# A new order, a slot of its own for the first y, deferred x loads and a second PSUM class for the last z in an eight-core decoder trunk

## The chip, the cores and the metric

The kernel runs on the eight cores of one Trainium2 chip. Each core works on its own share of the batch with no exchange between cores. The metric is the device time in microseconds (us) of the slowest core. TensorE, VectorE (DVE), ScalarE (ACT), GpSimd (POOL) and SyncE (SP) of a core each run their own instruction stream in order and meet at semaphores. POOL and SP also issue the transfers.

## The reference

Two layers, each on x with 1024 channels. A layer normalises x, multiplies by one wide input weight whose columns are seven groups, works on two head groups and adds an output product:

```
h  = rmsnorm(x, g)
a_val, a_gate, z_a, Bg, C, hb, z_b = split(h @ w_in)      # 7 x 1024 columns
u  = a_val * sigmoid(a_gate)                              # group A
ca = head_layernorm(causal_dwconv(u, width 31) + bias)    # per head of 128 channels
y_a = silu(ca) * silu(z_a)
v  = C * hb                                               # group B
y_b = Bg * causal_dwconv(v, width 3) * silu(z_b)
x  = x + concat(y_a, y_b) @ w_out                         # 2048 -> 1024
```

After layer 2 there is a final rmsnorm. Outputs are the x of the prompt and the samples, and the last rows of the inputs of both convolutions for every layer. The batch has 8 prompts of 2048 positions and 128 samples of 4 new positions.

## The kernel before, in words

Each core takes one prompt and 16 samples: 2112 columns, in four blocks of 512 (0 to 3) and block 4 of 64. Channels lie on partitions, x and h in eight chunks of 128. All products run on TensorE, with 128 x 128 weights against 512 (or 64) columns.

Per layer the work is split by head j: **P** is the GLU pair (value and gate), **C** the convolution of width 31 as Toeplitz matmuls (L1102, L1103) followed by the layer norm, **Z** the gate z_A, **a** the product C * hb of group B, **b** its gates Bg and z_B. ORDER lists them for each layer. "Z7up" is a Z whose y lies in a slot of the up_sb tile.

A product of two weight tiles over the four big blocks runs in one of two ways. *plain* makes eight times four matmuls for two weight tiles and two blocks. *pair* (line 984) is a Strassen-like scheme: seven products of four matmuls for the same, with sums of the weights (wsum) and of h (in xst) made beforehand, and copies and differences in PSUM (L1004, L1017) between them. STEPSP, STEPSa and STEPSb are the orders of these steps. WK lists the products of each layer that run as pairs; of those that it names, P0, P1 and a0 run block by block in the first loop all the same.

The first loop (line 1543 on) goes block by block through P0, P1 and a0, since block q's h only exists once x of that block has come and its squares are summed: rms_stat (line 763) squares on ACT (L783), either adds chunk pairs on DVE (L791) or, for the blocks in DIRECT, lets TensorE sum all chunks with a matrix of ones, and then goes through Ln (L806) and Exp (L820) on ACT and the h products on DVE (L869). Blocks 0 and 1 of layer 0 are RAW: they start on x that isn't normalised and are finished later (raw_finish, L850 and L852). In the rows this matrix is ones_s, the squares are tmp, and psb is any PSUM bank.

The convolution of head 0 needs u of P0: it is stored to DRAM (scr_u, L1045), read back in another layout (up_sb, L1060) and needs the last columns of the neighbour group (the halo copies on POOL, L1043) beforehand. The layer norm goes through DRAM too (scr_c, L1146, L1149). The last product of a layer is out_final: 16 tiles of w_out (256 KB each) are loaded by POOL into slots that earlier work frees, as HOMES gives them; output blocks come in the order OUTQ (in layer 1: block 4 of 64 columns, then 0, 1, 2, 3), each summed over 16 chunks of y in PSUM, then added to x on DVE (L1358). In layer 1 x comes back from x_mid in DRAM through SP (L1332). PSUM banks are shared by classes, CAPS: five for "proj", two for "conv", one for "z".

The order of the instructions is not written by hand. A list scheduler (class Sched) takes all operations with their resources, keys (BG shifts these by name), pools and PSUM classes, and writes an order for each engine, which the engines then follow. Weight tiles for products wait in a pool of slots (wsl). y has a pool of its own. x of the first loop lies in an area ("arena") in y_sb and xst, and a y may be written there once its readers are through.

Lines in the text are those of the profile of the kernel before. The matmul helper is L743, that of the pairs L996. In the new kernel the same lines are L748, L1001, and later ones move by 5 to 18.

Of the kernel before, what the change touches and what calls it, by code (L numbers as in the profile page):

```python
# [30 lines left out]
NB = 5  # L31
# [16 lines left out]
    "b0 C0 a1 C1 P2 C2 Z0 b1 P3 a2 Z1 P4 C3 C4 P5 Z2 b2 P6 a3 C5 b3 C6 Z3 P7 a4 Z4 Z5 b4 Z6 a5 C7 b5 a6 b6u0 a7 b7u1 Z7up",  # L48
    "b0 C0 a1 C1 P2 Z0 b1 C2 Z1 P3 a2 P4 C3 C4 P5 b2 Z2 P6 a3 b3 C5 Z3 a4 C6 Z4 Z5 b4 P7 a5 C7 b5 a6 b6 a7 Z6u0 b7u1 Z7up",
# [20 lines left out]
WK = ['P0 P1 P2 P3 P4 P5 P6 a0 a2 a3 a4 a5 a6 a7 b6 b7', 'P0 P1 P2 P3 P4 P5 P6 P7 a0 a1 a2 a3 a4 a5 a6 a7 b6 b7']  # L70
BG = {"sd": -300, "p5b": 30, "co": 30, "y": 300, "sz": -30, "halo": 30, "sdb": 100, "th": -30, "sub": -300, "c": 30, "s": 30, "sa": 100, "hist": -30, "wt": 30, "nrm": -30, "p": -300, "lsq": -300, "sb": -300, "u2": -30}
# [432 lines left out]
def build_nc():  # L504
# [35 lines left out]
    def sb(name, shape, dt):  # L540
# [222 lines left out]
    def rms_stat(part, pool=False, after=(), early=False, copy=False, raw=False, direct=False):  # L763
# [4 lines left out]
        for kp in range(4):  # L768
            s = V("snap")
            if q in SPLIT and raw and kp == 3:  # L770
# [553 lines left out]
    def x_stage(l, q):  # L1324
# [4 lines left out]
        for i, v in enumerate(x.vs):  # L1329
# [177 lines left out]
    for l in range(DEPTH):  # L1507
# [213 lines left out]
```

How the kernel before makes its waits and increments, by code:

```python
            def body(e):  # L482
                for o in self.order[name]:
                    for d in o.waits:
                        e.wait_ge(chan_sems[d.chan] if d.chan is not None else sems[d.eng], d.cnt)
                    ins = o.fn(e)
                    if o.chan is not None:
                        ins.then_inc(chan_sems[o.chan], 16)
                    elif o.sig:
                        ins.then_inc(sems[name], 1)
                if name == "sp":
                    for ch in final_chans:
                        if ch in cnt:
                            e.wait_ge(chan_sems[ch], cnt[ch])
```

## Time and profile before

| what | value |
|---|---|
| median of 3 runs | 1088.03 us (1087.13 to 1253.58) |
| the profiled execution | 1088.93 us, span 1087.4 us on the slowest core, core 7 |
| spans of all cores | 1078.9 to 1087.4 us, granted clock 0.995 to 0.998 |
| TensorE busy | 1054.1 us, 97% of the span, 7010 instructions |
| DVE, ACT, POOL busy | 751.3 us (69%), 630.0 us (58%), 311.0 us (29%) |
| bytes by DMA | 142.45 MB, mean 131 GB/s |

The profile was taken on the slowest core. A span runs from the first to the last instruction. What lies outside it is 1.5 us. TensorE's granted clock is in tenths or parts of its full speed (2.4 GHz); 0.50 is the lower of its two levels.

### The profile page before, as it was taken

What the parts mean: (1) busy time and instruction counts of PE and PEld (TensorE: products, weight loads), DVE (VectorE), ACT (ScalarE), POOL (GpSimd) and SP (SyncE); (2) the same over time, 40 slices, a digit from 0 to 9 for tenths busy, and PEclk for the clock granted to TensorE, in tenths of its full rate; (3) what the DMA queues carried; (4) which work ended last, traced back from release to release, by engine and by line L of the source; (5) the groups of instructions that cost most, each with busy time, mean ns of one, the idle gap of its engine ahead of it and who ended that gap; (6) DMA issues with size and microseconds to landing.
All of it is one profiled execution on the core that took longest, in us unless ns stands there. A gap on an engine that the chain in (4) does not pass through costs nothing.

```text
span 1087.4 us, 21321 instructions; the slowest of 8 cores (1078.9 to 1087.4 us)
## 1 busy us (share of the span) xinstructions
PE 1054.1 (97%) x7010; PEld 528.3 (49%) x7010; DVE 751.3 (69%) x1458; ACT 630.0 (58%) x1029; POOL 311.0 (29%) x470
## 2 busy tenths in 40 slices
PE   6989999999999999999999999999999999989997
PEld 3445455555544544444544445545455554444464
DVE  3768978778688887433555888788779788843332
ACT  5954777686777665121151568768577866533332
POOL 7462222222232222222151222222312222213341
PEclk9989999999999999999999999999999999999999
DMA  9927878869676759554433775885966765931454
GB/s 238 206 28 141 129 135 120 150 101 158 114 118 114 115 99 200 146 186 177 158 99 89 114 125 92 154 157 87 154 107 96 140 110 79 203 97 35 146 154 169
DMA packets 185803, 142.45 MB, mean 131 GB/s; under 512 B 140000, under 2 KB 152160, under 8 KB 185632
## 3 DMA queue, kind: packets, MB, share of 16 engines
q0 software_dynamic: 34352, 54.97, 33.8%
q1 hardware_dynamic: 150816, 82.17, 30.5%
q10 hardware_dynamic: 528, 3.96, 1.0%
q8 instruction: 58, 0.95, 0.4%
q14 instruction: 49, 0.40, 0.2%
HBM read 149.08 MB, written 43.79 MB: 177 GB/s over the span
## 4 chain that ended last, share of the span: by engine, by line
PE 90%; DMA 5%; POOL 1%; ACT 1%; issue 1%; DVE 1%; ACTq 0%; DVEq 0%; SPq 0%; POOLq 0%
PE psb L743 55%; PE psb L996 31%; DMA wsl<-w_in_r 2%; PE psb L1102 2%; PE psb L1103 2%; PE psb L1441 1%; DMA wsl<-w_out_r 1%; DMA big<-scr_c 1%; DMA scr_c<-big 1%; DMA xst<-x_mid 1%; POOL y_sb L1480 0%; DMA y_fm<-xst 0%; POOL toep L1521 0%; POOL wsl L722 0%; PE psb L1444 0%
## 5 line engine op out<-in xcount | busy, mean ns | idle before, releaser
L743 PE MATMUL psb<-h_sb,wsl 128*128 128x512 bf16 (+1 forms) x2272 | 364.4, 309 | 10.9 <-DVE h_sb L869 3.2
L743 PEld LDWEIGHTS psb<-h_sb,wsl 128*128 128x128 bf16 x2272 | 167.6, 98 | 181.5 <-issue 19.3
L1076 ACT ACTIVATE toep<-wt_sb 32x512 bf16<-32x512 bf16 x192 | 119.8, 625 | 33.5 <-PE psb L1103 21.5
L1358 DVE TENSOR_TENSOR xst<-xst,psb 128x512 f32<-128x512 f32 (+2 forms) x80 | 44.7, 566 | 123.5 <-PE psb L743 99.8
L783 ACT ACTIVATE tmp<-xst 128x1024 bf16<-128x1024 f32 (+2 forms) x44 | 38.6, 880 | 150.6 <-DVE xst L1358 140.9
L1285 DVE SCALAR_TENSOR_TENSOR tmp<-vbuf,cw_b_sb,tmp 128x512 f32<-128x512 bf16 (+1 forms) x160 | 108.0, 675 | 19.7 <-ACT tmp L1282 11.5
L996 PE MATMUL psb<-h_sb,wsl 128*128 128x512 bf16 x448 | 113.6, 379 | 0.4 <-ACT psb L1004 0.4
L996 PE MATMUL psb<-xst,wsum 128*128 128x512 bf16 x448 | 110.8, 379 | 1.3 <-DVE wsum L950 0.8
L996 PE MATMUL psb<-h_sb,wsum 128*128 128x512 bf16 x448 | 108.8, 379 | 1.0 <-DVE psb L1017 1.0
L722 POOL DMA_DIRECT2D wsl<-w_in_r x110 | 60.0, 552 | 166.9 <-PE psb L743 91.6
L1069 POOL DMA_DIRECT2D wt_sb<-wt_d x64 | 35.2, 551 | 214.1 <-DVE toep L1080 68.1
L791 POOL TENSOR_TENSOR tmp<-tmp 128x512 bf16<-128x512 bf16 (+2 forms) x40 | 37.4, 935 | 160.4 <-ACT tmp L783 160.3
L1282 ACT ACTIVATE tmp<-vbuf,cw_b_sb 128x512 f32<-128x512 bf16 (+1 forms) x80 | 51.4, 642 | 35.6 <-DVE y_sb L1315 30.1
L1107 DVE TENSOR_TENSOR big<-psb,cbt_sb 128x320 bf16<-128x320 f32 x128 | 62.3, 487 | 13.0 <-PE psb L1103 10.8
L1197 ACT ACTIVATE tmp<-big,vecs_sb 128x512 f32<-128x512 bf16 (+1 forms) x80 | 58.8, 735 | 19.9 <-DMA big<-scr_c 6.5
L743 PE MATMUL psb<-h_sb,wsum 128*128 128x512 bf16 (+1 forms) x288 | 68.3, 369 | 0.0
L743 PE MATMUL psb<-y_sb,toep 128*128 128x512 bf16 (+2 forms) x320 | 67.0, 333 | 0.0
L996 PEld LDWEIGHTS psb<-xst,wsum 128*128 128x128 bf16 x448 | 41.9, 98 | 48.0 <-issue 2.5
L743 PE MATMUL psb<-y_sb,wsl 128*128 128x512 bf16 (+2 forms) x280 | 59.9, 327 | 3.8 <-DMA wsl<-w_out_r 3.8
L996 PEld LDWEIGHTS psb<-h_sb,wsum 128*128 128x128 bf16 x448 | 41.3, 98 | 45.3 <-issue 2.1
L996 PEld LDWEIGHTS psb<-h_sb,wsl 128*128 128x128 bf16 x448 | 40.8, 98 | 42.8 <-issue 1.0
L743 PE MATMUL psb<-y_sb,wsum 128*128 128x512 bf16 (+2 forms) x280 | 60.6, 335 | 0.2 <-issue 0.2
(155 smaller groups left out, 1826.8 us busy)
## 6 DMA issues: line engine op xcount, KB each, us to landing
wsl<-w_in_r POOLq DMA_DIRECT2D x110, 256.0 KB, 5.7
scr_u<-u_sb SPq DMA_DIRECT2D x16, 704.0 KB, 6.8
up_sb<-scr_u SPq DMA_DIRECT2D x16, 704.0 KB, 7.5
scr_c<-big SPq DMA_DIRECT2D x16, 640.0 KB, 7.2
big<-scr_c SPq DMA_DIRECT2D x16, 640.0 KB, 6.1
wt_sb<-wt_d POOLq DMA_DIRECT2D x64, 128.0 KB, 4.0
xst<-x_d SPq DMA_DIRECT2D x16, 512.0 KB, 8.5
x_mid<-xst SPq DMA_DIRECT2D x16, 512.0 KB, 2.9
```

Of the source, the lines that this page charges most:

```text
L722: return e.dma_start(out=wsl[:, v.slot, :], in_=src)
L743: ins = e.matmul(bank(v, n), lhsT=l_(), rhs=r_(), start=(first and i == 0), stop=(last and i == len(pairs) - 1))
L783: act((lambda e, s=s, kp=kp: e.activation(out=tmh(s, 0, 2 * n).rearrange("p (k c) -> p k c", k=2), in_=x2(kp, part), func=AF.Square)), 2 * ...
L791: S.op("pool" if pool else "dve", (lambda e, s=s: e.tensor_tensor(out=tmh(s, 0, n), in0=tmh(s, 0, n), in1=tmh(s, n, n), op=ALU.add)), 0.15 ...
L996: ins = e.matmul(bank(v, 512), lhsT=lhs(k), rhs=rhs(k), start=first and k == 0, stop=True if not first else k == 3, skip_group_check=not f ...
L1069: pooldma((lambda e: e.dma_start(out=wt_sb[:, w.slot, :], in_=wt_d[l, j, qt])), 0.75, (), [w], f"wt{(j * 4 + qt) % 4}", pkt=0.09, name=f"w ...
L1076: act((lambda e, p=p, c=c: e.activation(out=toep[p, tp.slot, :].rearrange("p (m x) -> p m x", x=128)[:, :, 32 * c:32 * c + 32], in_=wt_sb[ ...
L1107: dve((lambda e, b=b, v=v, bias=bias: e.tensor_tensor(out=big[:, co.slot, 4 * b:4 * b + 4, :], in0=bank(v, 4 * CROW).rearrange("p (g c) -> ...
L1197: act((lambda e, s=s, q=q, n=n: e.activation(out=b4(tm(s, n), q), in_=c_blk(cn.slot, q), func=AF.Silu, scale=vecs[:, 16 + col:17 + col], b ...
L1282: act((lambda e: e.activation(out=b3(tm(a, n), q), in_=v_blk(q, 0), func=AF.Copy, scale=cw_b[:, l, j, 2:3])), n, [v_r[q], cwb_r], [a], ptr ...
L1285: dve((lambda e, lag=lag: e.scalar_tensor_tensor(out=b3(tm(a, n), q), in0=v_blk(q, lag), scalar=cw_b[:, l, j, 2 - lag:3 - lag], in1=b3(tm( ...
L1358: x_op[0] = dve((lambda e: e.tensor_tensor(out=x.s(m, part), in0=x.s(m, part), in1=bank(v, n), op=ALU.add)), n, [v, xr], [xr], holds=x.hol ...
```

## The change

ORDER, the step orders, the order of output blocks, of z blocks, and the scheduler's key offsets (BG) and the lists of pairs (WK) are replaced by others. Block 3 joins DIRECT: TensorE sums its squares. In layer 1 a0 leaves the first loop (FIRST) and becomes a pair in its ORDER. The first y of b0 gets a slot "e" of its own in y_sb that nothing of x uses; the pool of y has one slot less and x of block 4 moves to xst. In the last layer the x loads of the second output block (block 0) also wait for the last four w_out tiles of the list (XLW): two in wsum and two in big. The five z products of Z7 take their PSUM banks alternately from the classes z and conv. START puts w3 ahead of the x load of block 4, and w6 ahead of that of block 3.

```diff
--- before.py
+++ after.py
@@ -45,20 +45,20 @@
 ORDER = [
...
-    "b0 C0 a1 C1 P2 Z0 b1 C2 Z1 P3 a2 P4 C3 C4 P5 b2 Z2 P6 a3 b3 C5 Z3 a4 C6 Z4 Z5 b4 P7 a5 C7 b5 a6 b6 a7 Z6u0 b7u1 Z7up",
...
+    "C0 P1 a0 Z0 b0 a1 C1 P2 C2 Z1 P3 b1 a2 C3 P4 b2 P5 C4 Z2 Z3 P6 a3 b3 C5 C6 a4 Z4 P7 b4 Z5 C7 a5 b5 a6 Z6 b6u0 a7 b7u1 Z7up",
...
-STEPSb = "P11 P51 P50 P61 P10 P60 P20 P31 P71 P30 P21 s P41 P70 P40"
...
+STEPSb = "P10 P50 P11 P60 P51 P61 P20 P31 P71 s P21 P30 P41 P70 P40"
...
-OUTQ = (1, 2, 0, 4, 3)
+OUTQ = (0, 4, 2, 1, 3)
...
-ZQ = (2, 1, 4, 3, 0)
+ZQ = (3, 2, 0, 4, 1)
@@ -67,17 +67,20 @@
-WK = ['P0 P1 P2 P3 P4 P5 P6 a0 a2 a3 a4 a5 a6 a7 b6 b7', 'P0 P1 P2 P3 P4 P5 P6 P7 a0 a1 a2 a3 a4 a5 a6 a7 b6 b7']
+WK = ['P0 P1 P2 P3 P4 P5 P6 a0 a2 a3 a4 a5 a7 b0 b3 b6 b7', 'P0 P1 P2 P3 P4 P5 P6 P7 a0 a1 a2 a3 a4 a6 a7 b4 b7']
...
-DIRECT = (0, 1, 2, 4)
-
-START = "u0 u1 t0 t1 w0 w1 x1 w2 x4 w3 x2 w4 w5 x3 w6 w7"
+DIRECT = (0, 1, 2, 3, 4)
+
+FIRST = (('P0', 'P1', 'a0'), ('P0', 'P1'))
+XLW = 4
...
+START = "u0 u1 t0 t1 w0 w1 x1 w2 w3 x4 x2 w4 w5 w6 x3 w7"
...
-FINISH = {2: (0,), 3: (1,)}
+FINISH = {1: (0,), 4: (1,)}
@@ -583,7 +586,7 @@
-        "y": Pool(NY, spare=1),
+        "y": Pool(NY - 1, spare=1),
@@ -1167,6 +1172,8 @@
+            if self.place == "e":
+                return y_sb[:, NY - 1, a:b]
@@ -1175,9 +1182,10 @@
-    def proj_t(w, zs, q, **kw):
-        v = V("bank", "z", "full")
+    def proj_t(w, zs, q, cls="z", **kw):
+        v = V("bank", cls, "full")
@@ -1191,16 +1199,17 @@
-        for q in ZQ if j == 7 else range(NB):
+        for i, q in enumerate(ZQ if j == 7 else range(NB)):
             n = BLOCKS[q][1]
+            cls = "conv" if j == 7 and i % 2 else "z"
...
             if PAIRS and q in (1, 3):
-                bz = proj_t(w, zs, q, after=[cn_of[(l, j, "op")]], name=f"z{j}.{q}", **y.kw())
+                bz = proj_t(w, zs, q, cls, after=[cn_of[(l, j, "op")]], name=f"z{j}.{q}", **y.kw())
             else:
-                bz = proj(w, q, cls="z", after=[cn_of[(l, j, "op")]], name=f"z{j}.{q}", **y.kw())
+                bz = proj(w, q, cls=cls, after=[cn_of[(l, j, "op")]], name=f"z{j}.{q}", **y.kw())
@@ -1321,7 +1330,7 @@
-    def x_stage(l, q):
+    def x_stage(l, q, after=()):
@@ -1331,7 +1340,7 @@
                   1.9 * w / 1024, [] if l == 0 else [xmid_r[q][i]], x.res[2 * i:2 * i + 2] if q < 4 else x.res, f"xl{nx[0] % NX}",
-                  pkt=0.172 if q < 4 else 0.09, holds=[v], after=x_late if l == 0 else (), name=f"xl{q}.{i}")
+                  pkt=0.172 if q < 4 else 0.09, holds=[v], after=list(after) + (x_late if l == 0 else []), name=f"xl{q}.{i}")
@@ -1392,7 +1401,7 @@
             if part[1] == 0:
-                x_stage(l, part[0])
+                x_stage(l, part[0], [r.w for rr in wres[-XLW:] for r in rr] if final and n == 1 and XLW else ())
@@ -1511,7 +1520,7 @@
-            w_first = [w_load(w_in_r[l, c]) for c in (8, 0, 9, 1, 32, 40)]
+            w_first = [w_load(w_in_r[l, c]) for t, c in (("P0", 8), ("P0", 0), ("P1", 9), ("P1", 1), ("a0", 32), ("a0", 40)) if t in FIRST[l]]
@@ -1569,25 +1580,27 @@
-            y = Y()
+            y = Y("e")
...
-                y = Y(rest[1:] or None)
+                y = Y("e" if tok == "b0" else rest[1:] or None)
@@ -1605,7 +1618,7 @@
-            if not (tok == "b0" and w_b0):
+            if not (tok == "b0" and w_b0 or tok in w_of):
```


The new order at three places. The first is TensorE at the end of layer 0's first loop. Rows with ones_s sum the squares of block 3, the last in this loop. wsl holds weight tiles, wsum two of b0's weight tiles here. Before:

```order
L743 MATMUL psb<-h_sb,wsum 128x512 x8
L743 MATMUL psb<-h_sb,wsl 128x64 x24
L743 MATMUL psb<-tmp,ones_s 128x512
L743 MATMUL psb<-h_sb,wsum 128x512 x8
L743 MATMUL psb<-tmp,ones_s 128x512
L743 MATMUL psb<-h_sb,wsum 128x64 x16
L743 MATMUL psb<-h_sb,wsl 128x512 x48
L743 MATMUL psb<-h_sb,wsum 128x512 x48
L743 MATMUL psb<-h_sb,wsl 128x512 x20
L743 MATMUL psb<-h_sb,wsum 128x512 x4
```

Now:

```order
L748 MATMUL psb<-tmp,ones_s 128x512 x2
L748 MATMUL psb<-h_sb,wsl 128x512
L748 MATMUL psb<-h_sb,wsum 128x512 x16
L748 MATMUL psb<-h_sb,wsl 128x64 x8
L748 MATMUL psb<-h_sb,wsum 128x64 x8
L748 MATMUL psb<-h_sb,wsl 128x512 x2
L748 MATMUL psb<-h_sb,wsl 128x64 x8
L748 MATMUL psb<-h_sb,wsum 128x64 x8
L748 MATMUL psb<-h_sb,wsl 128x512 x46
```

Before, 16 matmuls of 64 columns stand between the last sum and the first products of block 3 (the row of 48). Now 17 of 512 columns and 16 of 64 stand there; then come the first two matmuls of block 3, 16 more of 64 columns, and the other 46.

The second is TensorE at the end of layer 1, from the last pair's matmuls (L996, in the new kernel L1001) on. The products from h_sb with zsum or wsl are z products (and some of block 4 of 64 columns); those from y_sb are the first output sums, of block 4, which read w_out tiles in toep, wsl and later slots. Before:

```order
L996 MATMUL psb<-xst,wsl 128x512 x4
L743 MATMUL psb<-y_sb,wsl 128x64 x4
L743 MATMUL psb<-y_sb,toep 128x64 x4
L743 MATMUL psb<-y_sb,wsl 128x64 x4
L743 MATMUL psb<-h_sb,wsl 128x64 x8
...
L743 MATMUL psb<-y_sb,wsl 128x64 x4
L743 MATMUL psb<-h_sb,wsl 128x512 x4
L743 MATMUL psb<-h_sb,zsum 128x512 x4
L743 MATMUL psb<-h_sb,wsl 128x512 x8
L743 MATMUL psb<-y_sb,wsl 128x64 x2
```

Now:

```order
L1001 MATMUL psb<-xst,wsl 128x512 x8
L748 MATMUL psb<-h_sb,wsl 128x512 x16
L748 MATMUL psb<-h_sb,wsl 128x64 x8
L748 MATMUL psb<-y_sb,toep 128x64 x4
L748 MATMUL psb<-y_sb,wsl 128x64 x4
...
L748 MATMUL psb<-y_sb,wsl 128x64 x4
L748 MATMUL psb<-h_sb,wsl 128x512 x4
L748 MATMUL psb<-h_sb,zsum 128x512 x4
L748 MATMUL psb<-y_sb,toep 128x64 x4
L748 MATMUL psb<-y_sb,wsl 128x64 x6
```

Behind the pair's last four matmuls there were 16 of 512 columns up to the row of y_sb, wsl x2, whose tile is the last one loaded; now there are 24, since the last two steps of the pair stand together ahead of 16 of them. The rows left out are of 64 columns.

The third is SP at the end of layer 1: the x loads (L1332, now L1341), the load of tail_d and the store of ob. Before:

```order
L1332 DMA xst<-x_mid 128x512
L1332 DMA xst<-x_mid 128x1024
L1614 DMA ob_d<-obt 128x272
L1332 DMA xst<-x_mid 128x1024 x2
L1409 DMA big<-tail_d 128x1152
L1332 DMA xst<-x_mid 128x1024 x2
L875 DMA y_fm<-xst 128x128 x4
```

Now:

```order
L1418 DMA big<-tail_d 128x1152
L1627 DMA ob_d<-obt 128x272
L1341 DMA xst<-x_mid 128x512
L1341 DMA xst<-x_mid 128x1024 x5
L880 DMA y_fm<-xst 128x128 x4
```

The load of tail_d and the store of ob come first now, and no x load stands between them.

## Rows read from the trace of the kernel before

**Rows 1.** The page's chain that ended last: share of the span by engine.

```profile
PE 90%; DMA 5%; POOL 1%; ACT 1%; issue 1%; DVE 1%; ACTq 0%; DVEq 0%; SPq 0%; POOLq 0%
```

**Rows 2.** Windows: stretch, length, busy us (instructions) of PE, PEld, DVE, ACT, POOL; clock; DMA.

```profile
0.00:70.00 70.00, 55.75 (x317) 26.45 (x318) 40.92 (x85) 52.58 (x77) 42.14 (x55) 0.95 0.71 173
70.00:945.00 875.00, 868.79 (x5909) 432.25 (x5907) 659.95 (x1277) 533.25 (x881) 229.69 (x374) 1.00 0.69 129
945.00:970.00 25.00, 18.51 (x196) 11.02 (x195) 13.59 (x29) 9.65 (x18) 2.64 (x8) 0.93 0.56 135
...
sum 1087.40, PE 1054.09 PEld 528.26 DVE 751.29 ACT 629.97 POOL 311.02; mean PE 263.52 PEld 132.06 DVE 187.82 ACT 157.49 POOL 77.76
```

**Rows 3.** Waits of TensorE: who waited for what; us in total, times, longest.

```profile
PE psb L743 <- DMA wsl<-w_out_r: 3.8, 1, 3.8
PE psb L743 <- DVE h_sb L869: 3.2, 1, 3.2
PE psb L743 <- ACT tmp L1205: 2.5, 2, 1.7
PE psb L743 <- DMA big<-scr_c: 1.6, 1, 1.6
```

**Rows 4.** Spans of the cores and their mean granted clock.

```profile
core 4: 1084.5 us, clock 0.997
...
core 7: 1087.4 us, clock 0.995
```

**Rows 5.** Timeline, first loop's end: start, busy us, engine, line, tiles, [idle before, releaser].

```profile
60.08 0.63 PE L743 MATMUL psb<-h_sb,wsum 128*128 128x64 bf16 x16
60.32 1.28 ACT L806 ACT_TABLE_LOAD   x1 [0.21 <-PE psb L743]
...
63.01 1.41 DVE L869 SCALAR_TENSOR_TENSOR h_sb<-xst,vecs_sb,psb 128x512 bf16<-128x512 f32 x2 [2.05 <-ACT psb L820]
...
63.91 0.59 PE L743 MATMUL psb<-h_sb,wsl 128*128 128x512 bf16 x1 [3.20 <-DVE h_sb L869]
```

**Rows 6.** Busy time in three short stretches, same columns.

```profile
60.00:65.00 5.00, 1.80 (x21) 0.94 (x19) 2.68 (x5) 4.67 (x7) 2.96 (x4) 0.80 0.00 0
65.00:70.00 5.00, 5.00 (x13) 1.78 (x12) 5.00 (x8) 4.28 (x8) 3.70 (x3) 0.52 0.01 3
960.70:964.10 3.40, 3.40 (x65) 3.40 (x66) 1.90 (x8) 0.62 (x2) 0.91 (x3) 0.50 0.02 5
```

**Rows 7.** Timeline of TensorE in the tail.

```profile
947.91 1.03 PE L996 MATMUL psb<-xst,wsl 128*128 128x512 bf16 x4
948.77 0.28 PE L743 MATMUL psb<-y_sb,wsl 128*128 128x64 bf16 x4
...
960.25 0.22 PE L743 MATMUL psb<-y_sb,wsl 128*128 128x64 bf16 x2 [3.76 <-DMA wsl<-w_out_r]
```

**Rows 8.** DMA issues of 944.2:949.6, then 933.9:934.55, 920.5:920.6: count, KB each, us to landing.

```profile
xst<-x_mid SPq DMA_DIRECT2D x2, 512.0 KB, 10.7
wsum<-w_out_r POOLq DMA_DIRECT2D x2, 256.0 KB, 11.5
wsl<-w_out_r POOLq DMA_DIRECT2D x1, 256.0 KB, 10.3
...
wsl<-w_out_r POOLq DMA_DIRECT2D x2, 256.0 KB, 6.9
...
wsl<-w_out_r POOLq DMA_DIRECT2D x1, 256.0 KB, 5.6
```

**Rows 9.** The first convolution: DMA issue on SP, its landing, TensorE's start.

```profile
85.88 0.37 SPq L1060 DMA_DIRECT2D up_sb<-scr_u  x1
...
up_sb<-scr_u SPq DMA_DIRECT2D x1, 704.0 KB, 7.5
...
97.90 0.20 PE L1102 MATMUL psb<-up_sb,toep 128*128 128x80 bf16 x1
```

**Rows 10.** DMA issues of 523.4:523.6, end of layer 0.

```profile
x_mid<-xst SPq DMA_DIRECT2D x1, 256.0 KB, 18.3
```

More of the change, by code:

```diff
@@ L625, in flat @@
                     return xst[:].rearrange("p a t -> p (a t)")[:, k * n:(k + m) * n]
-                lo = 4096 * self.q if self.q < 3 else 12288
+                if self.q == 4:
+                    return xst[:, 4, k * n:(k + m) * n]
+                lo = 4096 * self.q
                 return x0f[:, lo + k * n:lo + (k + m) * n]
@@ L783, in rms_stat @@
             act((lambda e, s=s, kp=kp: e.activation(out=tmh(s, 0, 2 * n).rearrange("p (k c) -> p k c", k=2), in_=x2(kp, part), func=AF.Square)),
-                2 * n, [xp(2 * kp, part), xp(2 * kp + 1, part)], [s], sbuf=True, tab=None, after=after, holds=hold(2 * kp), name=f"sq{q}.{kp}")
+                2 * n, [xp(2 * kp, part), xp(2 * kp + 1, part)], [s], sbuf=True, tab=None, after=after, holds=hold(2 * kp), name=f"{SI if x.first else 'sq'}{q}.{kp}")
             if direct:
@@ L1156, in __init__ @@
         def __init__(self, place=None):
-            self.res = rs(NB)
+            self.res = rs(NB) if place != "e" else e_r
             self.v = V("y") if place is None else None
             self.place = place
-            base = x0_arena if place is None else u_r[int(place[1])] if place[1] in "01" else [up_r, uph_r]
+            base = () if place == "e" else x0_arena if place is None else u_r[int(place[1])] if place[1] in "01" else [up_r, uph_r]
             self.after = [o for r in base for o in r.r + ([r.w] if r.w else [])]
-            if place is not None:
+            if place not in (None, "e"):
                 late_y[place] = self.res
@@ L1530, in build_nc @@
                     x_load(i, ("pool",))
-        wA, wB = w_first[:4], w_first[4:]
+        w_of = {t: (w_first[2 * i], w_first[2 * i + 1]) for i, t in enumerate(FIRST[l])}
         if l == 0:
@@ L1549, in build_nc @@
                 r = rms_stat(whole(nxt), after=[rms_stat.ln], raw=nxt in RAW, direct=nxt in DIRECT)
-            p1_block(l, 0, q, wA[0], wA[1], sp, cur)
-            p1_block(l, 1, q, wA[2], wA[3], sp, cur)
+            for j in range(2):
+                if f"P{j}" in w_of:
+                    p1_block(l, j, q, *w_of[f"P{j}"], sp, cur)
             if nxt in RAW:
@@ L1555, in build_nc @@
                 rms_apply(0, whole(nxt), r)
-            pb_a_block(l, 0, q, wB[0], wB[1], sp, cur)
+            if "a0" in w_of:
+                pb_a_block(l, 0, q, *w_of["a0"], sp, cur)
             if cur is not None:
@@ L1562, in build_nc @@
         if l == 0:
-            x0_arena[:] = [r for q in (0, 1, 2, 4) for r in xcur[q].res]
-            x_late[:] = [o for r in xcur[3].res for o in r.r + [r.w]]
+            x0_arena[:] = [r for q in (0, 1, 2) for r in xcur[q].res]
+            x_late[:] = [o for q in (3, 4) for r in xcur[q].res for o in r.r + [r.w]]
         else:
@@ L1571, in build_nc @@
             dve(lambda e: e.memset(vbuf[:, 0:2, :], 0.0), 160, (), [vh_r])
-        p1_end(l, 0)
-        p1_end(l, 1)
+        for j in range(2):
+            if f"P{j}" in w_of:
+                p1_end(l, j)
         up_load(l, 0)
-        pb_a_end(l, 0)
+        if "a0" in w_of:
+            pb_a_end(l, 0)
         pending = []
         if w_b0:
-            y = Y()
+            y = Y("e")
             pending.append((8, y))
@@ L1582, in build_nc @@
             t_forms(x_late)
-        seen = {"P0", "P1"}
+        seen = set(w_of)
         ups = [1]
@@ L1615, in build_nc @@
         last = l == DEPTH - 1
-        pending.sort(key=lambda cy: cy[1].v is None)
+        pending.sort(key=lambda cy: cy[1].place not in (None, "e"))
         assert len(pending) == 16
```

10 lines of the change are left out of this document (6 added, 4 removed).

## The prediction

> **What bounds the kernel now.** The chain of waits comes first [rows 1]: TensorE fills 90% of the span and DMA 5%, so time can be won almost only where TensorE stands idle or runs at half clock, or by taking matmuls out. The table by stretch [rows 2] tells how much that is: TensorE is busy 1054.1 of 1087.4 us. Of the 33.3 us of idle time 14.3 lie before 70 us, where the first x and weights arrive, 6.2 between 70 and 945, 6.5 in the 25 us after that. The list of waits [rows 3] names the ends of them: 3.8 us for a w_out tile, 3.2 for the h of block 3 (DVE L869), 2.5 for the SiLU of z (ACT L1205), 1.6 for the relayout of c. The spans of the cores [rows 4] say whose time counts: core 7's, 2.9 us longer than core 4's. The profiled execution took 1088.93 us, 1.5 more than its span and 0.9 more than the median of the runs (1088.03).
>
> **The change part by part.** The number of matmuls hardly moves: 28 products run as pairs before and after (the entries of WK that the first loop runs by block don't count), and the order has 7000 matmuls against 6996. The four more sum block 3's squares, which DVE L791 added before: 4 x 0.216 us = **+0.9** (four matmuls of 512 columns start at 947.91, the next group at 948.77 [rows 7], so 0.216 each; one of 64 columns is worth 0.0285).
>
> *The stall at the end of the first loop.* TensorE issues the last 16 matmuls of 64 columns at 60.08 and has nothing until 63.91 [rows 5], as the chain from the last sum of squares runs through a table load (60.32), Ln, Exp and DVE L869 (63.01): 3.83 us against 0.63 of matmuls. In the new order 17 matmuls of 512 columns and 16 of 64 stand between that sum and the first product that reads block 3's h: 17 x 0.216 + 16 x 0.0285 = 4.1 us. That covers the chain; but the h tiles come at DVE's 0.70 a tile (1.41 for two), and other work on DVE stands between them, which leaves some 0.7 of waiting: 3.2 - 0.7 = **-2.5**.
>
> *The clock behind it.* In 60 to 65 us the granted clock is 0.80 and in 65 to 70 it is 0.52 [rows 6]: TensorE ran at its 1.2 GHz level from about 64 to 70, directly behind the idle stretch. Six us at half clock cost 3.0. The fall follows the stall, so I take it back with it: **-3.0**, bounds 0 and -3.4 (0.68 x 5, both stretches).
>
> *The tail.* The last w_out tile goes into the slot that layer 1's last pair frees. The pair's last four matmuls start at 947.91, and the first matmul that needs the tile at 960.25, after a wait of 3.76 [rows 7]. The tile took 10.3 us, beside two x loads of 512 KB (10.7) [rows 8]. In the order before, 16 matmuls of 512 columns and 44 of 64 stand between the pair's end and that use, 4.7 us; now 24 and 48, 6.55. Also block 0's four x loads now wait for the two wsum tiles, so fewer loads share the DMA engines with the last one. In less crowded places the same transfer took 5.6 and 6.9 [rows 8]. With 0.7 from release to issue and 0.5 from landing to use, a tile of 5.6 is 0.2 us late, of 6.9 1.5, of 10.3 about 5. I take 0.2, since only the wsum pair and one x load are left beside it. The z stalls of 1.7 and 0.8 [rows 3] go too: the last z products now alternate between two classes of PSUM banks, so that one need not wait until the SiLU has emptied the other's; what is late next there is the SiLU itself, 0.5 at most. 3.76 + 2.5 - 0.2 - 0.5 = **-5.6**, ends -1.4 (tile as slow as before) and -6.3 (no wait left).
>
> By the Trainium skill ("DMA: Bandwidth & Descriptors", section Queues, rings and completion order) each DMA engine takes turns between the queues that have work. By that a tile that no longer shares with the x queue would land in half of 10.3, an estimate of 5.2, and the tail would give -5.8; the 5.6 of the less crowded row agrees with it, the 6.9 less so.
>
> The deferred x loads stay hidden. Issued when the wsum tiles land (11.5 us after an issue that comes 4.5 ahead of the pair's end), they are there 11.5 - 4.5 + 10.7 = 18 us after that end, 21 if each is 1.5 slower. TensorE stops for them only once five banks hold block 0's sums: 6.6 of cover, some 3 of 64-column sums and 5 x 16 x 0.216 = 17.3, together 26.
>
> *The clock in the tail* was 0.50 from 960.7 to 964.1 [rows 6], a loss of 1.7. It follows the longest wait there; **-1.5**, bounds 0 and -1.7.
>
> *The middle.* In layer 0 one z product waits 1.6 for its normalised c [rows 3], which goes through DRAM. By the order the fewest matmuls between the sums over a c and its z product are worth 16.1 us there, so the way takes 17.7; in the new order the fewest of all heads are worth 22.0: **-1.6**. The other small waits stay in kind, since one convolution and the next stand as close as before (13.1 us of matmuls, now 13.5).
>
> *The first convolution.* The relayout of u is issued at 85.88 and takes 7.5, so it landed at 93.4; the convolution starts at 97.90, a margin of 4.5 [rows 9]. The new order puts 91 matmuls of 512 columns between u's product and the convolution, not 111: 20 x 0.216 = 4.3 less, so the margin is gone; and POOL issues four weight loads, not three, ahead of the halo copies that the store of u waits for. Half a us for that issue and one for a fuller DMA: **+1.5**, between 0 and +5.1 (both transfers of u as slow as the 10.3 of [rows 8]).
>
> *At nothing.* Block 0's first y in a slot of its own: the last reader of x's arena, ACT L850, works in the first loop, and b0's products come after it. x of block 3 one weight tile later: its squares now end ahead of more matmuls than before. Layer 1's first loop without a0: the cover of each sum of squares falls from 32 to 22 us, still five times that chain [rows 5]. The store of ob and the load of tail_d change places with x loads on SP, and nothing on SP waits long for them.
>
> Sum: -2.5 - 3.0 - 5.6 - 1.5 - 1.6 + 0.9 + 1.5 = -11.8; 1088.9 - 11.8 = **1077 us**, for a profiled execution as for the runs within the 0.9 between them.
>
> **Rivals.** (1) *The tile's wait stays*, 14%: it needs 10.3 again and is 5 late, the clock falls behind it: 5.6 - 1.4 + 1.5 = 5.7 not won, 1083. For it speaks that the wsum tiles took 11.5 [rows 8]. (2) *The first loop's stall moves on*, 10%: TensorE waits 5 us for the first convolution instead of 1.5 and the clock falls there: 1077 + 3.5 + 3.0 = 1084. (3) *The middle gets new waits*, 10%: its idle time is 6.2 [rows 2] and the whole order is new; if it doubles, with 2 us of clock beside it, 1085. (4) *Slower*, 6%: u's relayout meets other transfers, as one of 256 KB took 18.3 us beside the copies of layer 0's end [rows 10], against 7.5 here. 10.8 later still, with 3.0 of clock: 1077 + 13.8 = 1091. It decides from 9 us of lateness beyond the sum's 1.5 on. Against it: nothing of such a copy runs near 90 us. (5) *No effect*, 5%: the pairs are 28 on both sides and the waits only change their names, 1088 to 1089. My forecast has 55%.
>
> A rule that speaks against the deferral stands in the Trainium skill, "DMA: Bandwidth & Descriptors", section Issuing engines are not separate DMA queues: all DMAs run on the same 16 engines, whoever issues them. By it the bytes of x are only moved; the price would be block 0's loads coming late, 18 to 21 us against the 26 above, so nothing.
>
> **Range and chances.** From 1070 (all bounds won, no wait at the convolution) to 1089 (rivals 1, 2, 3 and most of 5 inside). Faster by over 2%, about what a measurement of this kernel can tell from no change, needs less than 1066.3: 3%. Slower by 2% needs over 1109.8: 2%. Between: 95%.
>
> **What would show it.** After the change: no wait of TensorE for the h of block 3 over 1 us, and a clock of 1.00 from 60 to 70; the w_out wait under 1 us, with the last tile landing in 5 to 7; no wait for the relayout of c in the middle; 0 to 5 us of waiting for up_sb at the first convolution. I am wrong if that wait is over 5, if the last tile still needs 10, or if the idle time between 70 and 945 exceeds 12.

## The result, and the profile after

The changed kernel took 1075.99 us (median of 4 runs, 1075.59 to 1078.02) against 1088.03 us for the kernel before, run beside it (3 runs, 1087.13 to 1088.83): a ratio of 0.9893, 95% interval 0.9874 to 0.9913. Here and below, medians leave out the runs of a slower state that any of these kernels can fall into, in which a die's cores show a lower granted clock (1253.58 us for the kernel before). 1077 was forecast, with 1070 to 1089 as its range. The profiled execution took 1075.72 us; its slowest core is core 2 with 1074.2 us, core 7 follows with 1074.1. Since the rows of before are core 7's, those of after are taken from core 7 too, where nothing else is said.

The page's chain of waits, by engine, to be held against [rows 1]: the DMA share is down from 5% to 3%.

```profile
PE 89%; ACT 3%; DMA 3%; issue 2%; DVE 1%; POOL 1%; ACTq 0%; DVEq 0%; POOLq 0%; SPq 0%
```

The windows of core 7, columns as in [rows 2]:

```profile
0.00:70.00 70.00, 55.73 (x333) 26.61 (x334) 37.01 (x81) 51.16 (x75) 41.63 (x55) 1.00 0.71 173
70.00:945.00 875.00, 872.63 (x5962) 434.92 (x5961) 664.50 (x1289) 540.41 (x890) 230.05 (x376) 1.00 0.70 129
945.00:970.00 25.00, 24.76 (x200) 12.76 (x199) 12.16 (x31) 8.88 (x16) 6.50 (x9) 1.00 0.46 138
970.00:1074.10 104.10, 96.15 (x524) 51.69 (x522) 32.30 (x57) 31.23 (x49) 33.02 (x31) 0.98 0.44 132
```

Idle time of TensorE is length less busy. Before 70 us it is 14.3, as before, though the stall of 3.2 is gone from it; from 70 to 945 it is 2.4 in place of 6.2; in the 25 us behind that 0.2 in place of 6.5. Behind 970 us it has grown from 6.4 to 8.0; the row of the kernel before for this stretch, which [rows 2] leaves out, is:

```profile
970.00:1087.40 117.40, 111.04 (x594) 58.54 (x592) 36.84 (x69) 34.48 (x54) 36.55 (x34) 1.00 0.38 124
```

The clock of 0.98 there costs core 7 nothing: it falls only from 1070 us on, behind its last matmul. The waits of core 7, to be held against [rows 3]:

```profile
PE psb L748 <- ACT tmp L788: 10.4, 4, 7.1
PE psb L1450 <- DMA xst<-x_mid: 2.0, 1, 2.0
PE psb L748 <- DMA wsl<-w_in_r: 1.8, 1, 1.8
...
PE psb L748 <- ACT tmp L1214: 0.3, 1, 0.3
```

The w_out tile, L869 (now L874), the relayout of c and the z stall of 1.7 have no row any more; of the SiLU of z 0.3 are left. The largest rows are the first x (L788, at the program's start) and 2.0 for an x load at the end. Neither is new, and [rows 3] shows neither: on core 7 of the kernel before they were 7.8 (L783) and 1.0 (L1441).

```profile
PE psb L743 <- ACT tmp L783: 7.8, 4, 4.5
```

```profile
PE psb L1441 <- DMA xst<-x_mid: 1.0, 1, 1.0
```

The end of the first loop, granted clock in two windows, against [rows 6], and the timeline, against [rows 5]:

```profile
60.00:65.00 5.00, 4.93 (x51) 2.56 (x49) 3.16 (x5) 4.67 (x8) 2.31 (x3) 1.00 0.00 0
65.00:70.00 5.00, 4.88 (x23) 2.02 (x22) 5.00 (x10) 4.64 (x10) 3.94 (x4) 1.00 0.01 3
```

```profile
59.11 3.62 PE L748 MATMUL psb<-h_sb,wsum 128*128 128x512 bf16 x16
59.14 1.28 ACT L811 ACT_TABLE_LOAD   x1 [0.25 <-PE psb L748]
...
61.84 0.75 DVE L874 SCALAR_TENSOR_TENSOR h_sb<-xst,vecs_sb,psb 128x512 bf16<-128x512 f32 x1 [2.62 <-ACT psb L825]
...
63.03 0.60 PE L748 MATMUL psb<-h_sb,wsl 128*128 128x512 bf16 x2
```

Behind the last sum TensorE has 3.6 us of matmuls (59.11), and the same chain (table load at 59.14, the first h at 61.84) ends below them. At 63.03 the products of block 3 start with no idle time noted, and the clock stays at 1.00.

The tail, TensorE first, against [rows 7]; then the DMA issues of two windows, the last w_out tile (940.5 to 940.7) and the deferred x loads (943.4 to 945), against [rows 8]:

```profile
938.14 1.89 PE L1001 MATMUL psb<-xst,wsl 128*128 128x512 bf16 x8
939.87 3.85 PE L748 MATMUL psb<-h_sb,wsl 128*128 128x512 bf16 x24
...
946.62 0.34 PE L748 MATMUL psb<-y_sb,wsl 128*128 128x64 bf16 x6
```

```profile
wsl<-w_out_r POOLq DMA_DIRECT2D x1, 256.0 KB, 4.3
...
xst<-x_mid SPq DMA_DIRECT2D x4, 512.0 KB, 7.7
```

The pair's last matmuls are the eight at 938.14. The tile is issued at 940.58 and lands after 4.3 us, at 944.9; the six matmuls that need it come at 946.62 and wait for nothing. The x loads are issued 2.8 us behind it, at 943.42. On core 2 one matmul shows the wait that the forecast set at 1.5:

```profile
89.00 0.20 PE L1107 MATMUL psb<-up_sb,toep 128*128 128x80 bf16 x1 [1.35 <-DMA up_sb<-scr_u]
```

It is 1.35 us there and 1.0 on core 0; the other six cores show none.

### The profile page after: what moved, and what is told of

It is laid out like the page before. It is cut to its first block, busy times and chain, and to the rows that moved or that the text cites. A ratio compares the mean times of both kernels' runs of the same rounds, so it can differ in the third digit from the quotient of the medians.

```text
span 1074.2 us, 21175 instructions; the slowest of 8 cores (1070.1 to 1074.2 us)
## 1 busy us (share of the span) xinstructions
PE 1044.8 (97%) x6888; PEld 527.4 (49%) x7014; DVE 746.8 (70%) x1456; ACT 631.2 (59%) x1029; POOL 311.2 (29%) x470
## 4 chain that ended last, share of the span: by engine, by line
PE 89%; ACT 3%; DMA 3%; issue 2%; DVE 1%; POOL 1%; ACTq 0%; DVEq 0%; POOLq 0%; SPq 0%
PE psb L748 55%; PE psb L1001 30%; PE psb L1107 2%; PE psb L1108 2%; PE psb L1450 1%; DMA scr_u<-u_sb 1%; DMA wsl<-w_in_r 1%; DMA up_sb<-scr_u 1%; DMA y_fm<-xst 1%; ACT tmp L788 0%; ACT toep L1081 0%; ACT L1144 0%; PE psb L1453 0%; POOL toep L1530 0%; ACT tmp L893 0%
## 5 line engine op out<-in xcount | busy, mean ns | idle before, releaser
L748 PE MATMUL psb<-h_sb,wsl 128*128 128x512 bf16 (+1 forms) x2218 | 354.7, 305 | 4.0 <-DVE big L1112 0.8
L788 ACT ACTIVATE tmp<-xst 128x1024 bf16<-128x1024 f32 (+2 forms) x48 | 39.6, 832 | 137.8 <-DVE xst L1367 126.6
L1001 PE MATMUL psb<-h_sb,wsl 128*128 128x512 bf16 x426 | 109.8, 379 | 1.6 <-ACT tmp L1302 0.5
L1001 PE MATMUL psb<-xst,wsum 128*128 128x512 bf16 x438 | 109.1, 379 | 0.7 <-ACT psb L1009 0.2
L1001 PE MATMUL psb<-h_sb,wsum 128*128 128x512 bf16 x428 | 105.0, 379 | 1.8 <-DVE psb L1022 0.4
L748 PE MATMUL psb<-h_sb,wsum 128*128 128x512 bf16 (+1 forms) x299 | 72.0, 369 | 0.3
L1001 PEld LDWEIGHTS psb<-xst,wsum 128*128 128x128 bf16 x448 | 42.3, 98 | 47.3 <-issue 0.5
L1228 ACT ACTIVATE tmp<-psb 128x512 f32<-128x512 f32 (+1 forms) x78 | 38.6, 519 | 43.4 <-PE psb L1001 24.8
L1302 ACT ACTIVATE tmp<-psb 128x512 f32<-128x512 f32 (+1 forms) x80 | 40.4, 517 | 39.4 <-PE psb L748 33.0
L1001 PEld LDWEIGHTS psb<-h_sb,wsum 128*128 128x128 bf16 x448 | 41.2, 98 | 44.1 <-issue 1.6
L1001 PEld LDWEIGHTS psb<-h_sb,wsl 128*128 128x128 bf16 x448 | 41.2, 98 | 44.1 <-issue 0.8
```

The source lines that it names most:

```text
L748: ins = e.matmul(bank(v, n), lhsT=l_(), rhs=r_(), start=(first and i == 0), stop=(last and i == len(pairs) - 1))
L788: act((lambda e, s=s, kp=kp: e.activation(out=tmh(s, 0, 2 * n).rearrange("p (k c) -> p k c", k=2), in_=x2(kp, part), func=AF.Square)), 2 * ...
L1001: ins = e.matmul(bank(v, 512), lhsT=lhs(k), rhs=rhs(k), start=first and k == 0, stop=True if not first else k == 3, skip_group_check=not f ...
L1228: act((lambda e: e.activation(out=tm(th, n), in_=bank(bc, n), func=AF.Copy)), n, [bc], [th], tab=None, name=f"cc{j}.{q}")
L1302: act((lambda e: e.activation(out=tm(sz, n), in_=sv(v, n), func=AF.Silu)), n, [v], [sz], sbuf=v is sz, name=f"szb{j}.{q}")
```

## The experiments

All kernels ran with the kernel before beside them; ratios are to that. It took 1085.9 us beside the t runs, l3, c1, v1b and v2, and 1085.3 beside l1, l2, m1 and v1, against 1088.0 in the result, so times of different paragraphs, and expected times, are compared by the ratios. In the kernels made from the one before, x of block 4 lies in xst as in the changed one, which leaves the order of TensorE as it was.

**t1_defer**: before, with the deferral alone.

```diff
+XLW = 4
...
-                x_stage(l, part[0])
+                x_stage(l, part[0], [r.w for rr in wres[-XLW:] for r in rr] if final and n == 1 and XLW else ())
```

> The kernel before with the deferral alone: block 0's x loads of the last layer wait for the last w_out tiles in wsum and big (and x of block 4 lies in xst in the first loop); the order of TensorE is that of before but for four rows. Theory D (the x loads slow the last w_out tile): the tile lands in 4 to 6 us in place of 10.3, its wait of 3.8 goes, and the half clock behind it: 1083 to 1085. The z stalls of 1.7 and 0.8 stay. Theory C (it was the cover of matmuls that was too short, the tile is slow anyway): 9 to 10 us, a wait over 3 us, 1087 to 1089.

Measured 1081.86 us, ratio 0.9953 (0.9936 to 0.9970), 5.1 us of the 1088.0. The last w_out tile (issue at 948.71), and two rows of the waits on this kernel's slowest core:

```profile
wsl<-w_out_r POOLq DMA_DIRECT2D x1, 256.0 KB, 4.4
```

```profile
PE psb L748 <- DVE h_sb L874: 3.2, 1, 3.2
PE psb L748 <- ACT tmp L1214: 2.5, 2, 1.7
```

The tile took 4.4 us in place of 10.3, its wait is gone on this core, the slowest (0.7 and 0.8 are left on two others), and the other waits stay. That is theory D. Theory C, by which the cover was too short, is refuted: with the old cover the wait goes.

**t2_zclass**: before, with the two PSUM classes alone.

```diff
-        for q in ZQ if j == 7 else range(NB):
+        for i, q in enumerate(ZQ if j == 7 else range(NB)):
+            cls = "conv" if j == 7 and i % 2 else "z"
```

> The kernel before with the two PSUM classes for the last z tile alone. Theory D: the z stalls of 1.7 and 0.8 go, but the last w_out tile is not a moment earlier, so its wait grows from 3.8 to about 6: no gain, 1087 to 1089. The rival (the z stalls are lost time of their own): 2.5 faster, 1085.5, with a wait for the tile still near 3.8.

Measured 1086.47 us, ratio 1.0003 (0.9992 to 1.0014). The tile, the wait for it, and a window behind it:

```profile
wsl<-w_out_r POOLq DMA_DIRECT2D x1, 256.0 KB, 10.3
```

```profile
PE psb L748 <- DMA wsl<-w_out_r: 5.8, 1, 5.8
```

```profile
955.00:965.00 10.00, 8.77 (x109) 6.54 (x110) 3.50 (x12) 1.43 (x5) 1.85 (x6) 0.70 0.00 0
```

The z stalls of 2.5 are gone and the wait for the tile has grown from 3.8 to 5.8, with the clock at 0.70 behind it. A stall that stands ahead of a later one was worth nothing alone here.

**t3_both**: both edits.

> The kernel before with both: deferral and two PSUM classes. Theory D: both kinds of waits go and the clock stays up, 6 to 8 us: 1080 to 1082, more than the two single edits together if the z classes alone give nothing. Theory C: 1085 to 1087, with a wait for the last w_out tile over 3 us.

Measured 1080.65 us, ratio 0.9945 (0.9927 to 0.9962): 6.0 us of the 1088.0, the low end of theory D.

```profile
wsl<-w_out_r POOLq DMA_DIRECT2D x1, 256.0 KB, 5.9
```

```profile
PE psb L748 <- DMA wsl<-w_out_r: 1.5, 1, 1.5
```

The tile took 5.9 here and is 1.5 us late, since with the stalls gone it is needed sooner: its cover is the old one. Over the eight cores the wait for it is 0 to 2.3 us. In the changed kernel, with 24 matmuls of 512 columns ahead of the tile's use and not 16, no core has such a wait; the longer cover was not added to t3 alone.

The deferred loads wait for the two wsum tiles, not for this last one, and here they went out 0.4 us behind it, issued at 946.68:

```profile
947.09 3.50 SPq L1341 DMA_DIRECT2D xst<-x_mid  x5
```

So this tile was not free of the x queue. Over the cores of t1 and t3 it took 5.6 to 7.4 us where the x loads were issued within 0.35 us of it, and 4.0 to 4.4 where they came 1.3 us or more behind. In the kernel before it took 8.2 to 10.3: there the x loads were out first, and the two wsum tiles ahead of it in POOL's own queue, which took 11.5 on core 7 [rows 8] and 4.0 to 4.4 here, had not landed when it was issued.

**t4_no_defer**: the changed kernel without the deferral.

```diff
-XLW = 4
+XLW = 0
```

> The changed kernel without the deferral: block 0's x loads wait only for their slots; TensorE's order differs only behind the first output sums. Theory D: the last w_out tile takes 8 to 10 us beside the x loads against 4.3, its wait is 2 to 4 us, with some half clock behind it: 1078 to 1082. Theory C: the 6.6 us of matmuls that now stand ahead cover it: within 1 us of the changed kernel's 1076.

Measured 1082.2 us (1080.26 to 1083.15), ratio 0.9956 (0.9939 to 0.9974).

```profile
wsl<-w_out_r POOLq DMA_DIRECT2D x1, 256.0 KB, 8.6
```

```profile
PE psb L748 <- DMA wsl<-w_out_r: 2.7, 1, 2.7
```

```profile
945.00:955.00 10.00, 7.00 (x110) 5.52 (x109) 6.35 (x16) 3.75 (x9) 1.64 (x4) 0.83 0.23 64
```

With the same matmuls ahead of it the tile takes 8.6 us, is 2.7 late, and the clock falls to 0.83 in the window. Theory C is refuted in the new order too. By the ratios the deferral is worth 6 to 7 us in the changed kernel, more than the 2 to 6 that theory D gave it. The profiled execution, 1080.26, is 4.3 over the changed kernel, about what the wait and 1.7 us for ten at 0.83 make; the other three took 1.5 to 2.9 us more, and where they lost it stays open.

**l1_first_loop**: before, with the first loop's part.

```diff
-DIRECT = (0, 1, 2, 4)
-START = "u0 u1 t0 t1 w0 w1 x1 w2 x4 w3 x2 w4 w5 x3 w6 w7"
-FINISH = {2: (0,), 3: (1,)}
+DIRECT = (0, 1, 2, 3, 4)
+START = "u0 u1 t0 t1 w0 w1 x1 w2 w3 x4 x2 w4 w5 w6 x3 w7"
+FINISH = {1: (0,), 4: (1,)}
```

> The kernel before with the first loop's part alone: block 3's squares summed by TensorE, the new START and FINISH; behind the last sum TensorE then has 17 matmuls of 512 columns and 32 of 64, as in the changed kernel, and the tail is that of before. Theory L (the stall was a lack of matmuls behind the last sum, and the half clock follows the stall): the wait for L869's line under 0.7 us, clock 1.00 from 60 to 70, 0.9 us more matmuls, 0 to 1.5 of wait at the first convolution: 3 to 5.5 us faster than the kernel before. Rival: the stall moves to the first convolution and takes its half clock with it: within 1.5 us of before.

Measured 1109.24 us, ratio 1.0217 (1.0199 to 1.0235): outside both. Four windows:

```profile
60.00:65.00 5.00, 4.71 (x48) 2.27 (x48) 5.00 (x8) 4.76 (x9) 2.95 (x3) 1.00 0.01 3
65.00:70.00 5.00, 5.00 (x25) 2.24 (x24) 3.75 (x9) 4.61 (x10) 5.00 (x5) 1.00 0.00 0
430.00:440.00 10.00, 2.72 (x13) 1.04 (x11) 7.08 (x10) 2.61 (x4) 0.53 (x1) 0.85 1.06 238
440.00:450.00 10.00, 1.37 (x4) 0.58 (x5) 0.00 (x1) 0.00 (x0) 0.53 (x1) 0.50 0.83 158
```

In the place that it was made for, the edit does what theory L says: clock 1.00 from 60 to 70, no wait for L874. Most of what is lost is lost at the end of layer 0, where TensorE stands, for 13.2 to 15.9 us on every core, and then runs at half clock. The wait on the slowest core, 6, and the DMA issues from 424 to 433 us:

```profile
PE psb L748 <- DMA big<-w_out_r: 15.9, 1, 15.9
```

```profile
big<-w_out_r POOLq DMA_DIRECT2D x4, 256.0 KB, 14.6
xst<-x_d SPq DMA_DIRECT2D x2, 512.0 KB, 12.3
wsum<-w_out_r POOLq DMA_DIRECT2D x2, 256.0 KB, 18.1
```

The kernel before issues its four tiles for big from 403 to 409 us and gets them in 8.3:

```profile
big<-w_out_r POOLq DMA_DIRECT2D x4, 256.0 KB, 8.3
```

The scheduler had put the last head of layer 0 later: its c is normalised at 410.02 here, at 393.25 before.

```profile
410.02 1.49 DVE L1149 TENSOR_TENSOR big<-big,rstd_h 128x2560 bf16<-128x2560 bf16 x1 [0.31 <-ACT rstd_h L1146]
```

```profile
393.25 1.49 DVE L1144 TENSOR_TENSOR big<-big,rstd_h 128x2560 bf16<-128x2560 bf16 x1 [0.57 <-ACT rstd_h L1141]
```

So the slots came free late, and six w_out tiles went out among the x loads, the last of the four for big at 432.56, just as TensorE began to wait. What in the scheduler's choices put the head later was not tried.

**l3_loop_defer0**: l1, with the same deferral at the end of layer 0.

```diff
-x_stage(l, part[0], [r.w for rr in wres[-XLW:] for r in rr] if final and n == 1 and XLW else ())
+x_stage(l, part[0], [r.w for rr in wres[4:8] for r in rr] if not final and n < 2 else ())
```

> The kernel of l1 (before with the first loop's part) and one more edit: at the end of layer 0 the x loads of the first two output blocks wait for the four w_out tiles that go into big. In l1 those tiles were issued at 424 to 433 us among six x loads, took 12 to 16 us and TensorE waited 15.9 for them, with half clock behind it: 1109. Theory (sharing the DMA engines is what makes the tiles late, as in the tail): they land in 5 to 9 us, the wait falls to 2 to 6, and 8 to 15 us come back: 1094 to 1101. Rival (they are issued too late, and the crowd costs little): 1105 to 1110.

Measured 1097.33 us, ratio 1.0105 (1.0085 to 1.0125), 12 us under l1.

```profile
big<-w_out_r POOLq DMA_DIRECT2D x4, 256.0 KB, 9.0
```

```profile
PE psb L748 <- ACT tmp L1214: 5.5, 5, 1.7
...
PE psb L748 <- DMA h_sb<-w_out_r: 3.0, 1, 3.0
...
PE psb L748 <- DMA wsl<-w_out_r: 2.7, 1, 2.7
```

The tiles for big land in 9.0 in place of 14.6, and no wait for them is left on any core; POOL issues them in l1's order and as late (the last at 431.58). So this is the mechanism of the tail, shown a second time and elsewhere. The 11 us over the kernel before that remain lie in several waits, of which the rows show the three largest at the ends of the layers; one of 3.0 stands in the first loop (DVE L911).

**l2_no_direct**: the changed kernel, DIRECT without block 3.

```diff
-DIRECT = (0, 1, 2, 3, 4)
+DIRECT = (0, 1, 2, 4)
```

> The changed kernel with block 3's squares added in pairs by DVE again. Behind the last sum stand 8 matmuls of 512 and 32 of 64 columns, 2.6 us, for a chain of 3.8. Theory L: a stall of 1.2 to 1.6 us at block 3's h, 0.9 us of matmuls less, the clock perhaps lower for 2 to 4 us: 0 to 2.5 us slower than the changed kernel, 1076 to 1078.5. Rival (the direct sums are only 0.9 us of extra work): 1075.

Measured 1075.68 us, ratio 0.9908 (0.9889 to 0.9926), which can't be told from the changed kernel's 0.9893 (0.9874 to 0.9913).

```profile
PE psb L748 <- DVE h_sb L874: 1.3, 2, 1.1
```

```profile
60.00:65.00 5.00, 3.57 (x29) 1.48 (x29) 4.10 (x7) 4.88 (x9) 2.69 (x3) 1.00 0.00 0
65.00:70.00 5.00, 5.00 (x25) 2.25 (x23) 3.69 (x8) 4.68 (x9) 5.00 (x4) 1.00 0.01 3
```

A stall of 1.1 us is back, 0.9 us of matmuls are gone, and the clock stays at 1.00 (on all eight cores). So the sums on TensorE take away the last 1.1 us of the stall and cost about as much. What shortened it from 3.2 and removed the half clock is not DIRECT. Nor is it ORDER: the next run has the new ORDER without START, FINISH and DIRECT, and keeps 3.2, while l1 has these three under the old ORDER and loses the stall. That leaves START and FINISH (after which block the raw blocks 0 and 1 are finished), which set what stands behind the last sum; the two were not run apart.

**m1_order**: before, with ORDER, STEPS, OUTQ, WK, BG and FIRST of the change.

> The kernel before with the new ORDER, step orders, OUTQ, lists of pairs, key offsets and FIRST (a0 of layer 1 out of its first loop), without the parts of the first loop, the z order, the classes and the deferral. Theory: the wait for the relayout of c (1.6) and some of the small waits go, 1 to 3 us; the stall at block 3's h stays near 3 us (0.7 us of matmuls behind the last sum) and the last w_out tile stays slow: ratio to before 0.997 to 0.999. Rival (the new order by itself is what closes the tail too): a wait for the last w_out tile under 1 us and a ratio of 0.993 or less.

Measured 1109.32 us, ratio 1.0219 (1.0197 to 1.0241): outside both as well.

```profile
PE psb L748 <- ACT tmp L1214: 8.4, 9, 1.9
PE psb L748 <- DMA big<-w_out_r: 7.6, 1, 7.6
...
PE psb L748 <- DVE h_sb L874: 3.2, 1, 3.2
```

No wait for the relayout of c has a row over 1 us, as the theory says, and the stall at block 3's h is there (3.2). But the tiles for big are late at the end of layer 0 as in l1, if by half as much (7.6), and the waits for z's SiLU sum to 8.4, with one PSUM class for z; other waits and half clock make up the rest of the 24 us. In the tail the last w_out tile is slow, as the theory says (9.1 us on this core), but its wait is 1.1, and 0 to 1.2 over the cores: the longer cover, and two z stalls of 1.1 and 1.2 ahead of it, gave it time. Like the parts of l1, these orders lose time alone and not in the whole.

**v1_x_in_h**: the changed kernel, and x of block 3 in the last layer goes to h_sb, ahead of its turn. The edit makes the loads wait for the last x add of block 1 (`xo[2]`), not of block 0 as the expectation has it: they are issued at 1006.49, and that add starts at 1005.73.

```diff
+            if self.home:
+                return h_sb[:].bitcast(F32)[:, k * n:(k + m) * n]
...
+        x = xcur[q] = X(q, home=home)
+        for i in range(4 if home else 0):
+            spdma(... out=h_sb[:].bitcast(F32)[:, 1024 * i:1024 * i + 1024] ..., after=list(after), ...)
...
+                x_stage(l, part[0], ... else [xo[2]] if final and n == 4 else (), final and n == 4)
```

> The changed kernel with one more edit: in the last layer x of block 3 is loaded into h_sb, free by then, behind block 0's last x add, and not into slots that stores of y_fm have to free first. In the changed kernel TensorE waits 1.2 to 2.5 us for these loads at about 1050 us on each core looked at. Theory: that wait goes, 1 to 2.5 us faster than the changed kernel: 1073.5 to 1075. Rival: the loads share the DMA engines with the stores of block 0 and 1 and something else waits: 1076 as the changed kernel.

Measured 1072.62 us, ratio 0.9883 (0.9861 to 0.9905). Core 7 of the changed kernel, then of this one, window 1050 to 1060:

```profile
1050.00:1060.00 10.00, 8.01 (x46) 4.64 (x45) 2.15 (x6) 2.45 (x5) 2.00 (x3) 1.00 0.41 98
```

```profile
1050.00:1060.00 10.00, 10.00 (x56) 5.76 (x55) 4.69 (x11) 3.68 (x10) 1.59 (x3) 1.00 0.31 105
```

2.0 us of idle time are gone from that window. By the ratios that is 1.1 us under the changed kernel, inside both intervals, so the two ran again beside each other.

**c1_changed** and **v1b_x_in_h**, the changed kernel and v1 again:

> The changed kernel itself, on the chip and in the rounds of the next two, to compare them with it: a ratio to before of 0.989 to 0.991.

> The same kernel as v1: x of block 3 of the last layer in h_sb. Theory: 1.5 to 3 us under the changed kernel of this call, a ratio of 0.987 to 0.989. Rival (v1's 1072.6 was the chip): no more than 0.5 under it.

Measured 1074.9 (ratio 0.9896, 0.9878 to 0.9914) and 1072.62 us (0.9875, 0.9858 to 0.9892). That is 2.3 us between the medians, and v1's highest run here, 1073.30, is below the changed kernel's lowest, 1074.29: v1 beats both kernels. The gain is not the wait alone. On the slowest core of the changed kernel in the result, core 2, the wait at this place is 2.3, here for a store that frees the slots:

```profile
PE psb L1453 <- DMA y_fm<-xst: 2.3, 1, 2.3
```

Behind it the clock is 0.83 from 1050 to 1060; on core 4, the slowest in c1's profile, a wait of 2.2 is followed by the same 0.83. In v1 and v1b all eight cores have 1.00 and hardly any idle time there.

**v2_x_in_h_no_direct**: v1, DIRECT without block 3.

> v1 and, as in l2, block 3's squares added by DVE again. Both saved something by themselves or nothing: l2 was 1075.7 against the changed kernel's 1076.0. Theory (0.9 us less work against a stall of 1.1): the same as v1 within 0.7 us. Rival: 0.9 less, the stall hidden by what waits elsewhere.

Measured 1073.3 us, ratio 0.9880 (0.9860 to 0.9900): 0.7 over v1b's 1072.62, on the edge of what the theory allows, and their runs overlap (1072.88 to 1073.71, and 1072.60 to 1073.30).

## Why the prediction was right

Core 7's span went from 1087.4 to 1074.1, 13.3 us; the sum said 11.8.

| term | forecast | core 7 |
|---|---|---|
| stall at block 3's h | -2.5 | -3.2 |
| half clock behind it | -3.0 | -3.0 (all of it gone) |
| waits in the tail | -5.6 | -6.2 |
| half clock in the tail | -1.5 | -1.7 (all of it gone) |
| idle time from 70 to 945 | -1.6 | -3.8 |
| block 3's sums | +0.9 | +0.9 (by count) |
| first convolution | +1.5 | 0 (1.4 on core 2, the slowest) |
| first x and weights | 0 | +3.2 |
| x loads at the end | 0 | +1.3 |

Core 7's terms come to -12.5, 0.8 short of what its span lost. The kernel's time went from core 7 of one to core 2 of the other, where the wait at the convolution is 1.4 and the one at the end 2.3 with half clock behind it.

The **stall** fell to nothing, not to 0.7: the other 16 matmuls of 64 columns stand behind the first two products of block 3 and cover the later h tiles. The forecast counted the sum on TensorE as part of the cure; l2 shows that it takes away only the last 1.1 us of it, for 0.9 us of matmuls.

The **clock** terms held as the sum put them, for the slowest core, and l1 shows that the half clock goes with the stall: 1.00 from 60 to 70. Its size was the step with the weakest ground: after the same stall the kernel before ran its next 5 us at 0.52 on core 7 [rows 6], at 0.66 to 0.87 on six cores and at 1.00 on core 0.

The **tail** rested on the landing time, taken as 5.6 to 6.9 from less crowded rows. It was 4.3, and the tile was there 1.7 us ahead of its use. With the deferral it needed 4.4, 5.9 and 4.3 (t1, t3, changed), without it 10.3, 10.3 and 8.6 (before, t2, t4). That the deferral does this is shown; that it is sharing with the x queue alone, which the forecast priced at half, is not. The tile was also freed of the two wsum tiles ahead of it in its own queue, which had themselves been slowed, and in t3 it had the x loads beside it for most of its 5.9. By the Trainium skill ("DMA: Bandwidth & Descriptors", section Queues, rings and completion order) each DMA engine takes turns between the queues that have work, from which the forecast had its estimate of 5.2. The rows lie around that number, but for the reason just given they are no clean test of it. By the Trainium skill ("DMA: Bandwidth & Descriptors", section Issuing engines are not separate DMA queues) all DMAs run on the same 16 engines, whichever engine started them. The forecast took from it that the bytes of x are only moved, and that held: the deferred x loads took 7.7 at the median, and no matmul of core 7 waited for them.

The **middle** is the mis-sized term: it counted one wait of 1.6 and let the others stand, and 3.8 went. The waits of pairs on DVE and ACT (L1017, L1004, L950: 2.7 together before, 0.8 after), which were to stay "in kind", mostly went; the forecast had looked at covers of convolutions only. m1 has none of these rows over 0.2 either, so they went with the new orders as a whole; the step orders were not run by themselves.

The **first convolution** came out at its value where it occurs. On core 7, whose first x came late, there is none.

**Not foreseen** were two. One is the program's start: the longest wait for the first x is 3.7 to 6.5 us on the eight cores before and 3.8 to 7.1 after, and POOL's issues differ only from 9.3 us on. So the +3.2 is mostly the spread between cores, and not the change. The other is the wait of 1 to 2.5 us for x of block 3 at the end, which was 0.4 to 2.6 before and which v1 takes away; the forecast's list of idle time stopped at 970 and never looked at the 6.4 us behind it. The two cost core 7 4.5 us, the middle gave 2.2 more than forecast and the first convolution 1.5; so the sum came out well in part by luck: misses of both signs met.

The **slot of its own** for the first y was put at nothing. It was not run by itself; without it the scheduler writes the same order for every engine, row for row.

Of the rivals none came: the tile's wait is gone, no stall at the convolution is above 1.4, there are no new waits in the middle and no slow relayout. What could have made it slower is another thing than the fourth rival: l1 and m1, each with a part of the change, take some 24 us more, in l1 mostly and in m1 in part (a wait of 7.6) through late w_out tiles at the end of layer 0, a place that the forecast never named. The whole change has no such wait there.

## What to carry to other kernels

A weight tile can be late through the company that it is issued in, as it was at two places here. Look at the other queue and at what stands ahead in its own, hold back the loads that nobody needs yet until it has landed, and price it with the landing time of a quiet row. A stall ahead of another is worth only what the second doesn't take back, so cure the last one first. Parts of an order need not be worth anything by themselves (l1, m1): measure the whole.

## What the runs showed of the hardware

The same 256 KB took 4.1 to 5.1 us on the eight cores of the changed kernel, where the loads of the other queue came 2.2 us or more behind; 5.6 to 7.4 with such loads issued within 0.35 us of it (t1, t3); 8.2 to 10.3 with such loads out first and two tiles of its own queue ahead (before); and 18.1 at the median for two of six tiles that went out together among such loads (l1). Half clock followed stalls of 3.2 us on most cores and for different lengths. Stalls of 2.0 to 2.8 in t4 were followed by 0.83 on five cores and by 1.00 on three. Stalls of 1.1 were followed by 1.00 on all eight cores (l2).
